# A two-block layer on one core: the chunks of a matmul operand are put 260 elements apart in SBUF in place of 256

## The reference

```
first block:   h = rmsnorm(x) * norm_pre_w
               proj = h @ w_in            # q k v o z (2048 columns each), 16 gate columns, u zb (1024), ga gb (2048)
               q, k = silu(causal conv(q, k));  h_a = mLSTM heads(q, k, v, gates);  y_a = h_a * sigmoid(o) * silu(z)
               y_b  = pooled(u) @ pool_w * silu(zb)
               out  = (sigmoid(ga) * (y_a @ w_proj_mlstm) + sigmoid(gb) * (y_b @ w_proj_pool)) @ w_out
               x1   = x + rmsnorm(out)
second block:  16 meta tokens put in front (272 tokens), rmsnorm, proj = hn @ w_in_2,
               differential attention and latent attention, gates, @ w_out_2, residual, rmsnorm
```

## Time and profile before

| | |
|---|---|
| median of 3 runs | 1538.94 us (1538.54 to 1539.81) |
| span of the profiled execution, first to last instruction | 1535.6 us |
| instructions in the profile | 27938 |
| PE matmul busy | 1496.3 us, 97% of the span, 10912 matmuls |
| DVE busy / ACT busy | 835.1 us (54%) / 711.4 us (46%) |
| mean granted TensorE clock | 0.994 of full speed |

### The profile page before, as it was taken

The page is one execution under the profiler, slowest core; times in us unless marked ns, Lnnn a source line. Parts: engine busy times, 40 slices in busy tenths (PEclk is TensorE's granted clock), DMA queues, the critical chain, the costliest instruction groups (busy, mean ns, idle before and its releaser), DMA issues.

```text
span 1535.6 us, 27938 instructions
## 1 busy us (share of the span) xinstructions
PE 1496.3 (97%) x10912; PEld 1415.4 (92%) x10912; DVE 835.1 (54%) x1028; ACT 711.4 (46%) x931; POOL 65.3 (4%) x90
## 2 busy tenths in 40 slices
PE   7999999999999999999999999989999999999997
PEld 7999998899999999999999998868999997888886
DVE  4667664545646555545454544555444444556754
ACT  5454445445454433433433434445433344666542
POOL 0000000101000000000000001000000001111000
PEclk9999999999999999999999999999999999999999
DMA  7565555655455555665565566646655553333563
GB/s 266 169 199 175 174 174 176 201 157 162 152 157 185 176 162 170 180 184 184 179 184 184 178 186 232 212 138 203 197 161 168 170 160 97 100 106 110 194 215 126
DMA packets 70647, 265.02 MB, mean 173 GB/s; under 512 B 7840, under 2 KB 7840, under 8 KB 69280
## 3 DMA queue, kind: packets, MB, share of 16 engines
q1 hardware_dynamic: 69552, 254.45, 53.4%
q0 software_dynamic: 1024, 9.57, 1.7%
HBM read 259.79 MB, written 4.19 MB: 172 GB/s over the span
## 4 chain that ended last, share of the span: by engine, by line
PE 94%; DVE 2%; ACT 2%; DMA 1%; issue 1%; DVEq 0%; POOL 0%; ACTq 0%; POOLq 0%
PE ps L299 23%; PE ps L303 23%; PE ps L301 23%; PE ps L289 5%; PE ps L291 5%; PE ps L290 5%; PE ps L398 1%; PE ps L406 1%; DMA metan<-in_meta 1%; PE ps L636 1%; PE ps L470 1%; PE ps L478 1%; PE ps L643 1%; PE ps L641 1%; PE ps L502 0%
## 5 line engine op out<-in xcount | busy, mean ns | idle before, releaser
L1078 DVE TENSOR_TENSOR wl<-raw,wh 128x1024 fp32r<-128x1024 f32 x474 | 579.9, 1227 | 572.2 <-ACT wh L784 564.8
L784 ACT ACTIVATE wh<-raw 128x1024 fp32r<-128x1024 f32 x474 | 499.4, 1059 | 564.7 <-PE ps L303 443.2
L299 PE MATMUL ps<-xh,wh 128*128 128x256 f32 x1792 | 510.4, 285 | 1.6 <-DVE xl L1091 1.6
L303 PE MATMUL ps<-xh,wl 128*128 128x256 f32 x1792 | 507.0, 283 | 0.0
L301 PE MATMUL ps<-xl,wh 128*128 128x256 f32 x1792 | 507.0, 283 | 0.0
L299 PEld LDWEIGHTS ps<-xh,wh 128*128 128x128 f32 x1792 | 343.9, 192 | 2.0 <-DVE xl L1091 1.8
L301 PEld LDWEIGHTS ps<-xl,wh 128*128 128x128 f32 x1792 | 343.9, 192 | 0.3
L303 PEld LDWEIGHTS ps<-xh,wl 128*128 128x128 f32 x1792 | 343.8, 192 | 0.0
L299 PE MATMUL ps<-x2h,wh 128*128 128x256 f32 (+1 forms) x688 | 198.8, 289 | 3.5 <-ACTq L897 3.3
L303 PE MATMUL ps<-x2h,wl 128*128 128x256 f32 (+1 forms) x688 | 195.2, 284 | 0.0
L301 PE MATMUL ps<-x2l,wh 128*128 128x256 f32 (+1 forms) x688 | 195.1, 284 | 0.0
(11 more groups left out here) (321 smaller groups left out, 1794.0 us busy)
## 6 DMA issues: line engine op xcount, KB each, us to landing
raw<-in_w_stream SPq DMA_DIRECT2D x474, 512.0 KB, 3.7
xn<-in_x SPq DMA_DIRECT2D x2, 1024.0 KB, 6.0
xr<-in_x POOLq DMA_DIRECT2D x1, 2048.0 KB, 16.1
x_kept<-xr POOLq DMA_DIRECT2D x1, 2048.0 KB, 9.5
x1r<-x_kept POOLq DMA_DIRECT2D x1, 2048.0 KB, 10.5
out<-yn SPq DMA_DIRECT2D x4, 512.0 KB, 2.7
const<-in_const SPq DMA_DIRECT2D x1, 1044.0 KB, 12.4
poolw<-in_pool_w POOLq DMA_DIRECT2D x1, 1024.0 KB, 5.5
```

Source lines behind the costliest of these rows:

```text
L299: pe.matmul(out_at(j), wh[r][:, c, f], hi[:, kc, tokens], start=st, stop=False, skip_group_check=True)
L303: last = pe.matmul(out_at(j), wl[r][:, c, f], hi[:, kc, tokens], start=False, stop=z, skip_group_check=True)
L784: act.activation(wh[r][:, :, :], raw[r][:, :, :], ACT.Copy).then_inc(wh_done, 1)
L1078: tt(wl[r][:, :, :], raw[r][:, :, :], wh[r][:, :, :].bitcast(F32), ALU.subtract).then_inc(split_done, 1)
```

## The change

The tiles get four more elements in each chunk, and everything that reads or writes them keeps its first 256 of 260. A chunk then starts 1040 bytes behind the last one in place of 1024. `xl` moves from 16384 to 17408 bytes behind `xh`, since `xh` has grown to 16640 bytes. Both fit into the room before `R_C`. Nothing else is changed: the same instructions in the same order with the same waits.

```
+XPITCH = S + 4
...
-    xh = sb("xh", [P, KC, S], F32R, R_X)
-    xl = sb("xl", [P, KC, S], F32R, R_X + 16384)
+    xh = sb("xh", [P, KC, XPITCH], F32R, R_X)[:, :, 0:S]
+    xl = sb("xl", [P, KC, XPITCH], F32R, R_X + 17408)[:, :, 0:S]
```

## The result

The changed kernel takes **1527.43 us** (median of 4 runs, 1525.65 to 1528.79) against 1538.74 us (4 runs): ratio **0.9933**, 95% interval 0.9919 to 0.9947, so 11.3 us less by the medians and 8.2 to 12.5 us by the interval. A repetition with six further runs gave 1527.77 us beside 1535.62 us in 13 runs of the kernel before, ratio 0.9938 (0.9920 to 0.9956); those medians are 7.9 us apart. Forecast were 1527.4 us, by a shorter step of PE's matmuls.

The account below looks back on a forecast made before the run. PE's instructions, one after the other, were taken as the bound. By-feature matmuls -13.4 and V +1.9 gave -11.5 us: span 1535.6 to 1524.1, plus 3.3 to the median, 1527.4 us (0.75% less), range 1511 to 1542 us.

Parts of the forecast that it names:

- PE's chain is the time, and the step from start to start is the cost: Whole kernel: PE busy 97% of the span and 94% of the chain; matmul steps, not their overlapping durations, cost time.
- The step depends on the chunk's place: By-feature matmuls: the step depends on where in SBUF the moving chunk starts, 120.0 ns at 256 pitch, 117.5 at 272.
- 117.5 ns as the mean over the 16 places: 5376 by-feature matmuls with `xh` or `xl` moving: mean step falls from 120.0 to 117.5 ns, saving 13.4 us.
- The four-place sum: Step readings at starts 128, 192, 0 and 64, (120 + 118.3 + 118.3 + 113.8) / 4, give 117.6 ns.
- V at 5.0 ns more, +1.9 us: Stage V, 384 matmuls with `xh` and `xl` stationary: each step 5.0 ns longer, costing +1.9 us.
- Writes, gate columns, stream: nothing: ACT's 32 chunk writes (below 0.3 us), 48 gate matmuls (0.1 us either way) and weight transfers: no cost counted.
- The 3.3 us between span and median: Whole kernel: the median of the runs stands 3.3 us above the profiled span, added to 1524.1 for the forecast.
- The slower rival: Moving chunks starting off a multiple of 64 bytes cost extra, 4032 matmuls: +18.7 us, 1557.7 us; chance 15%.
- No difference: Moving chunks: 16-byte steps don't leave the slow place, only V's 0 to 1.9 us left, 1538.9 to 1540.8; 13%.
- The larger gain: By-feature matmuls: in-between places are like the 113.8 ns chunk, mean step 115 ns, 25.0 us saved, 1513.9 us; 12%.

Follow-up runs that it names:

- e4: Kernel before with weights `wh` and `wl` moved up 64 bytes, from 128 to 192 in the 256-byte cycle, no activation moved within it: 1514.54 us, ratio 0.9850.
- e1: Kernel before, pitch still 256 elements, `xh` and `xl` moved up 192 bytes so every chunk starts at 64 in the 256-byte cycle: 1509.95 us, ratio 0.9820.
- the second kernel over the places: Kernel before, pitch 256, most x groups reading chunks at differing 16-byte offsets (second set of places), so results are other numbers: 1517.35 us, one run.
- e3: Kernel before with chunks of `xh` and `xl` 272 elements apart, starting at 128, 192, 0 and 64 in turn: 1526.79 us, ratio 0.9939.
- e2: Kernel before, pitch still 256 elements, `xh` and `xl` moved up 16 bytes, to 144 in the 256-byte cycle: 1524.33 us, ratio 0.9914.
- e9: Kernel before with `wh` and `wl` moved up 144 bytes, from 128 to 16 in the 256-byte cycle, no activation moved within it: 1543.03 us, ratio 1.0045.
- e8: Kernel before, pitch still 256, `xh` and `xl` moved up 112 bytes so every chunk starts at 240 in the 256-byte cycle: 1506.91 us, ratio 0.9807.
- e11: Kernel before, pitch 256, high and low tiles of x, y, z and cq all starting at 240, weights still at 128: 1496.86 us, ratio 0.9735.
- e7: Kernel before with only `xl` given the pitch of 260, `xh` kept at 256: 1529.46 us against 1538.37, one run each.

## Why the prediction was right

- *PE's chain is the time, and the step from start to start is the cost.* Right: the stage table puts the gain where `xh` and `xl` are the moving operand, nothing in the second block, and no new wait of PE.
- *The step depends on the chunk's place.* Right as far as it went. It depends on the place of both operands (e4), and one set of addresses can settle at different steps (e1, the loop of the second kernel over the places). The prediction named the stationary tiles' place and did not ask what it does.
- *117.5 ns as the mean over the 16 places.* Measured 117.6. The x stages gave 12.4 us for 13.4. The 117.5 was measured over 190 steps of AQ and carried over well. The four-place sum beside it mixed two kinds of reading, settled ends (120 for chunk 7, 113.8 for chunk 6) and whole chunks (118.3 for chunks 8 and 9; chunk 7 as a whole, 1198.87 to 1200.29 in the earlier trace rows, takes 118.3 too), and it doesn't hold place by place: place 192 was read as 118.3 and was 113.5 in the changed kernel. That the finer places have the same mean as the coarse ones was assumed, and e3 bears it out.
- *V at 5.0 ns more, +1.9 us.* Measured +1.8: the mean step of all its matmuls is 231.4 ns against 226.8.
- *Writes, gate columns, stream: nothing.* No stage shows them; ACT waits for PE as before.
- *The 3.3 us between span and median* was wrong. In every execution whose span is on record the time is the span and some 1.8 us. By that the trace of the kernel before is of an execution of 1537.4 us, none of the three runs it was said to be one of, and 1.5 of the 3.3 us are the difference of that execution from the median. For the changed kernel the median stands 0.4 us above the trace's span. The span itself fell by 8.6 us in place of 11.5, for WO's half clock, the 0.8 us at the start and 0.9 us less from the stages that the change touches. The two errors, 2.9 us each, have opposite signs and cancel: that the median hit the forecast within 0.1 us is luck. What the change gives is the stages' 10.6 us, for 11.5 forecast, and the repetition's ratio gives 9.5 us.
- *The slower rival* (off a multiple of 64 bytes costs extra) fell for the moving operand with the result itself, twelve of whose sixteen places are such starts, and with e2 and e3. For the stationary tiles e9 leaves it open: nothing was gained by a start of 16 where a gain was due. *No difference* fell with the result. *The larger gain* was wrong for this change, but its premise, that a place with 113 ns exists, carries e8 and e11: held there, the step saves 6.4 ns and not 2.4.
- The Trainium skill's page "Advanced Engine Details and Errata", section "SBUF Cachelines", asks for at least two hits on each 16-byte line and says nothing of where a read starts, so that by it the prediction had either pitch alike. It does not describe this: all places tried start on a whole line and are read in order, and the settled steps go from 113.3 to 120.0 ns.

**Still open:** what in the hardware couples the two operands' places, what picks among the steps of one set of addresses, why the weights at 16 don't behave like x at 240, and whether the executions without a kept trace settle as the ones with it. e1's traced execution took 1515.54 us, its others 1507.79 to 1510.59. The clock is not the reason for all of it, since that of 1507.79 us has the same granted clock, 0.994. QK at the fast step there would fit; no record shows it.

## What to carry to other kernels

Where PE is the bound and each weight tile serves one short matmul, look at the start-to-start step in the timeline, and compare it between stages of the same form: a difference of a few ns with no wait between is worth as much as a wait. Then shift the whole tile, by some multiples of 16 bytes, and keep the place at which every group is fast: a held place can be fast in one group and slow in the next, so one group is not enough to judge by; padding the pitch, as the change did, only averages over the places (0.993 here, against 0.981 for the same tiles held at place 240 and 0.9735 with `y`, `z` and `cq` there as well). Check the stages in which the same tile is the other operand, since they can pay for it.

## What the runs showed of the hardware that was not expected

- Matmuls of 256 float32r columns with a weight load each settled at steps of 113.3 to 120.0 ns at full clock, by the start addresses of both operands within 256 bytes (moving tiles alone took the kernel to 0.9735 of its time, e11). With 512 columns by token it was 226.7 to 233.3 ns.
- One loop body on one set of addresses settled at 113.4 ns in one turn and 117.7 ns in another. With held places a settled step changed only across a gap of 200 ns or more between the x matmuls (e1, e2, e4, e9). Place 144, held, had 118.7, 116.7 and 113.3 ns in one execution (e2).
- Moving the operand of every third matmul alone shortened the steps behind all three (-1.6, -0.5 and -2.2 ns, e7).
